# HGRN-2 stage of a hybrid decoder step on one core: projection units placed between the small matrix steps, v in three parts, forget gate and logarithms further forward

## The reference, cut to what matters

```
q, f, v, gate = jnp.split(x @ w_in, 4, axis=-1)
forget = lb + (1.0 - lb) * jax.nn.sigmoid(f)
log_f = jnp.log(forget)
k = (1.0 - lb) * jax.nn.sigmoid(-f)
q = jax.nn.silu(q)
# for each chunk of 16 steps and each of 16 heads:
G = jnp.cumsum(gc, axis=1)
qg = qc * jnp.exp(G)
att = einsum('blhd,bshd->bhls', qg, kc * jnp.exp(-G)), causal
o = einsum('bhls,bshv->blhv', att, vc) + einsum('blhd,bhdv->blhv', qg, S)
S = S * jnp.exp(g_last)[..., None] + einsum('bshd,bshv->bhdv', kc * jnp.exp(g_last - G), vc)
# then
o = rms_norm over the head, * norm_g * silu(gate);  y = o @ w_out
```

## Time and profile before

| what | value |
|---|---|
| median of 3 runs | 2430.7 us (2428.47 to 2439.7) |
| the profiled execution | 2442.74 us |
| its span, first to last instruction | 2440.8 us |
| PE busy | 2236.6 us, 92% of the span |
| DVE, ACT, POOL busy | 1270.4, 982.4, 1247.6 us |
| chain that ended last | PE 64%, DVE 18%, DMA 6%, ACT 5% |
| mean granted TensorE clock | 0.896 |
| stretch of groups i = 1 to 7 of HGRN | 1249.31 to 1692.28 us, 63.3 us a group |

### The profile page before, as it was taken

The page is one execution under the profiler, slowest core; times in us unless marked ns, Lnnn a source line. Parts: engine busy times, 40 slices in busy tenths (PEclk is TensorE's granted clock), DMA queues, the critical chain, the costliest instruction groups (busy, mean ns, idle before and its releaser), DMA issues.

```text
span 2440.8 us, 37825 instructions
## 1 busy us (share of the span) xinstructions
PE 2236.6 (92%) x14852; PEld 2017.3 (83%) x14852; DVE 1270.4 (52%) x2173; ACT 982.4 (40%) x1585; POOL 1247.6 (51%) x1565
## 2 busy tenths in 40 slices
PE   6898998789999999898899999999899889989987
PEld 5888996688899987796698889888799579889966
DVE  5798334146666674434245555555324338982342
ACT  3677432423344432342433322332243247764422
POOL 4798880343344442580363333444386049988702
PEclk8999999878899997899898888888799899999998
DMA  3434466233333323366223333332456624445660
GB/s 110 149 119 130 167 206 215 71 109 108 91 114 119 109 90 107 111 219 230 85 83 106 106 106 95 100 104 85 129 173 198 217 79 133 133 131 170 194 233 31
DMA packets 329760, 321.35 MB, mean 132 GB/s; under 512 B 21512, under 2 KB 311216, under 8 KB 329584
## 3 DMA queue, kind: packets, MB, share of 16 engines
q1 hardware_dynamic: 328720, 318.60, 41.1%
q10 hardware_dynamic: 864, 0.34, 0.1%
HBM read 289.27 MB, written 29.61 MB: 131 GB/s over the span
## 4 chain that ended last, share of the span: by engine, by line
PE 64%; DVE 18%; DMA 6%; ACT 5%; issue 3%; POOL 1%; SPq 1%; ACTq 0%; DVEq 0%
PE ps L669 10%; PE ps L670 9%; PE ps L674 9%; PE ps L1200 4%; PE ps L659 3%; PE ps L679 3%; PE ps L660 2%; PE ps L661 2%; PE ps L1076 2%; DMA work<-cache_mem_v 2%; PE ps L1246 2%; DVE work L2064 2%; PE ps L937 2%; DVE work L1914 2%; PE ps L946 2%
## 5 line engine op out<-in xcount | busy, mean ns | idle before, releaser
L1396 POOL TENSOR_TENSOR wl<-raw,wh 128x256 fp32r<-128x256 f32 x1536 | 1243.1, 846 | 1158.1 <-ACT wh L1419 1157.0
L669 PE MATMUL ps<-Hh,wh 128*128 128x320 f32 (+1 forms) x1536 | 490.2, 335 | 57.4 <-DVE Hl L1960 26.5
L1419 ACT ACTIVATE wh<-raw 128x1024 fp32r<-128x1024 f32 (+1 forms) x400 | 400.2, 1021 | 335.4 <-DMA raw<-hg_w_in 86.6
L670 PE MATMUL ps<-Hl,wh 128*128 128x320 f32 (+1 forms) x1536 | 474.6, 325 | 0.0
L669 PEld LDWEIGHTS ps<-Hh,wh 128*128 128x128 f32 x1536 | 317.2, 207 | 82.0 <-issue 48.2
L670 PEld LDWEIGHTS ps<-Hl,wh 128*128 128x128 f32 x1536 | 318.6, 207 | 1.3
L1914 DVE TENSOR_SCALAR work<-ps 128x512 f32<-128x512 f32 (+9 forms) x248 | 116.1, 486 | 276.0 <-PE ps L1092 56.2
L674 PE MATMUL ps<-Hh,wl 128*128 128x320 f32 (+1 forms) x1536 | 255.3, 309 | 2.5 <-POOL wl L1396 2.5
L674 PEld LDWEIGHTS ps<-Hh,wl 128*128 128x128 f32 x1536 | 234.1, 194 | 3.6 <-POOL wl L1396 3.6
L659 PE MATMUL ps<-Oh,wh 128*128 128x320 f32 x512 | 168.5, 329 | 8.4 <-POOL wl L1396 4.1
L669 PE MATMUL ps<-Oh,wh 128*128 128x320 f32 x512 | 161.4, 328 | 3.7 <-DVE Ol L2607 3.7
(11 more groups left out here) (398 smaller groups left out, 4127.4 us busy)
## 6 DMA issues: line engine op xcount, KB each, us to landing
raw<-rg_w_in SPq DMA_DIRECT2D x128, 256.0 KB, 3.7
work<-cache_mem_k SPq DMA_DIRECT2D x64, 512.0 KB, 4.8
work<-cache_mem_v SPq DMA_DIRECT2D x64, 512.0 KB, 5.9
raw<-hg_w_in SPq DMA_DIRECT2D x128, 256.0 KB, 5.0
raw<-ssd_w_in SPq DMA_DIRECT2D x96, 256.0 KB, 3.8
raw<-rg_w_out SPq DMA_DIRECT2D x64, 256.0 KB, 3.6
raw<-x_w_k SPq DMA_DIRECT2D x64, 256.0 KB, 3.6
raw<-x_w_v SPq DMA_DIRECT2D x64, 256.0 KB, 5.3
```

The costliest lines, as they stand in the source:

```text
L669: pe.matmul(ps[:, bank, 0:n], high(half, k), mh[:, k, 0:n], start=(k == 0), stop=False)
L670: pe.matmul(ps[:, bank, 0:n], high(half, k), ml[:, k, 0:n], start=False, stop=False)
L1396: ins = pool.tensor_tensor(out, src, wh[:, n % HALVES, r:r + 2].bitcast(F32), ALU.subtract)
L1419: act.activation(wh[:, n % HALVES, 0:rows], raw[:, slot, 0:rows, half * P:(half + 1) * P], ACT.Copy).then_inc(hi_ready, 1)
```

## The change

PE's loop for i = 1 to 7 is written anew; the steps of the last pass (i = 8) keep their order. The two units of f are taken apart and stand on either side of `outputs(j, 0)`, ahead of `turn_and_score(j, 1)`. v is taken in three parts, behind `gain(j, 0, 1)`, `gain(j, 1, 0)` and `outputs(j, 1)`. On ACT the copy `s1_copy(j, 1)` goes behind the logarithm and behind the splits of the next group's g units. On DVE `forget(i)` goes ahead of `turned(j, 1)`, and `sums_of_logs(i)` ahead of `last_state(j, 1)`. No instruction is added or removed, and POOL's and SP's lists are the same.

```diff
-                def take_f(i):
+                def take_f(i, half):
                     pe.wait_ge(*past("hg_g_read", i + 1))
-                    project(gfv(i), 0)
-                    project(gfv(i) + 1, 1)
-
-                def take_v(i):
-                    pe.wait_ge(*past("hg_f_read", i + 1))
-                    halves(2)
+                    project(gfv(i) + half, half)
+
+                def take_v(i, T):
+                    if T == 0:
+                        pe.wait_ge(*past("hg_f_read", i + 1))
+                        halves(2)
                     both, rest_of = pair(), pair_low()
...
-                    done(mm, 2)
+                    if T == 2:
+                        done(mm, 2)
...
-                for i in range(1, GROUPS + 1):
-                    last = i == GROUPS
...
-                        take_g(i)
-                        take_q(i, 0)
-                    turn_and_score(i - 1, 0)
...
-                        take_q(i, 1)
-                    states(i - 1, 0)
-                    gain(i - 1, 0, 0)
-                    outputs(i - 1, 0)
-                    turn_and_score(i - 1, 1)
-                    gain(i - 1, 0, 1)
...
-                        take_f(i)
-                    states(i - 1, 1)
-                    gain(i - 1, 1, 0)
-                    outputs(i - 1, 1)
-                    if not last:
-                        take_v(i)
-                    gain(i - 1, 1, 1)
-                    sums(i - 1)
+                for i in range(1, GROUPS):
+                    j = i - 1
+                    take_g(i)
+                    take_q(i, 0)
+                    turn_and_score(j, 0)
+                    take_q(i, 1)
+                    states(j, 0)
+                    gain(j, 0, 0)
+                    take_f(i, 0)
+                    outputs(j, 0)
+                    take_f(i, 1)
+                    turn_and_score(j, 1)
+                    gain(j, 0, 1)
+                    take_v(i, 0)
+                    states(j, 1)
+                    gain(j, 1, 0)
+                    take_v(i, 1)
+                    outputs(j, 1)
+                    take_v(i, 2)
+                    gain(j, 1, 1)
+                    sums(j)
...
                     act.activation(hg_k, ps[:, a:a + 2, 0:NT], ACT.Sigmoid, scale=-1.0).then_inc(S("hg_f_read"), 1)
-                    if i:
-                        s1_copy(i - 1, 1)
                     act.preload_act_table_set(EXP_SET)
                     act.wait_ge(*past("hg_forget", i + 1))
                     act.activation(hg_f, hg_f, ACT.Ln).then_inc(S("hg_logf"), 1)
                     ahead(b + 6)
+                    if i:
+                        s1_copy(i - 1, 1)
                     act.wait_ge(*past("hg_G_ready", i + 1))
...
+                    if i < GROUPS:
+                        forget(i)
+                    if i:
                         turned(i - 1, 1)
                         new_state(i - 1, 0, 1)
                         blocks_of_v(i - 1, 1)
                     if i < GROUPS:
-                        forget(i)
+                        sums_of_logs(i)
                     if i:
                         last_state(i - 1, 1)
-                    if i < GROUPS:
-                        sums_of_logs(i)
-                    if i:
                         gated(i - 1, 1)
                         new_state(i - 1, 1, 0)
```

More of the change, by code:

```diff
@@ L1040, in take_q @@
                     project(qs(i) + half, half)
-                def take_f(i):
+                def take_f(i, half):
                     pe.wait_ge(*past("hg_g_read", i + 1))
-                    project(gfv(i), 0)
-                    project(gfv(i) + 1, 1)
-                def take_v(i):
-                    pe.wait_ge(*past("hg_f_read", i + 1))
-                    halves(2)
-                    both, rest_of = pair(), pair_low()
[L1051 to L1056, removed]
-                    done(mm, 2)
+                    project(gfv(i) + half, half)
[3 more added lines that the diff above has]
+                        halves(2)
+                    both, rest_of = pair(), pair_low()
+                    t0 = (0, P, NT - P)[T]
+                    out = ps[:, gfv(i) + T // 2, 256 * (T % 2):256 * (T % 2) + 256]
+                    for k in range(KD):
+                        for n, (x, w) in enumerate(((Hh, both), (Hh, rest_of), (Hl, both))):
+                            mm = pe.matmul(out, x[:, k, t0:t0 + P], w(k), start=(k == 0 and n == 0), stop=(k == KD - 1 and n == 2))
+                    if T == 2:
+                        done(mm, 2)
                 def turn_and_score(i, h):
@@ new lines, in hg @@
+                take_f(0, 0)
+                take_f(0, 1)
+                for T in range(3):
+                    take_v(0, T)
+                for i in range(1, GROUPS):
[19 more added lines that the diff above has]
+                    sums(j)
@@ new lines, in hg @@
+                pe.wait_ge(*past("hg_q_read", GROUPS))
+                take_out(0, 0)
+                take_out(0, 1)
+                turn_and_score(7, 0)
+                pe.wait_ge(*past("hg_v_read", GROUPS))
+                take_out(0, 2)
+                states(7, 0)
+                gain(7, 0, 0)
+                outputs(7, 0)
+                turn_and_score(7, 1)
+                gain(7, 0, 1)
+                take_out(0, 3)
+                states(7, 1)
+                gain(7, 1, 0)
@@ L1164, in hg @@
+                outputs(7, 1)
+                gain(7, 1, 1)
+                sums(7)
                 pe.wait_ge(*past("hg_o_read", GROUPS * 2))
```

14 lines of the change are left out of this document (removed).

## The result

| | before | after |
|---|---|---|
| median (range), us | 2435.2 (2428.47 to 2441.24) | 2478.14 (2469.12 to 2479.4) |
| profiled execution, us; span | 2442.7; 2440.8 | 2476.97; 2475.1 |
| groups 1 to 7, a group | 63.28 us | 67.83 us |

The changed kernel is slower: the ratio is 1.0149, with a 95% interval of 1.0117 to 1.018. The two sides were run in turn on one chip, so its median of before is not quite that of the table ahead of the prediction. The span of the profiled execution grew by 34.3 us, and 31.8 of them lie in groups 1 to 7.

A forecast was written before the change was run, and what follows sets the result against it. PE, busy 92% of the span, was taken as the bound, through waits and stretches at 1.2 GHz. 38.5 + 28.7 = 67.2 us a group against 63.28, times seven 27 us more: 2458 us, range 2434 to 2490.

The forecast's parts named there:

- The mechanism: Before head 1's outputs PE idles 6 to 9 us for ACT's copy behind two splits; outputs then run at clock 0.50.
- The DMA chain: SP's head 0 state store, next load and g block: 10.9 us from store to ACT's first split.
- Second part: Group from head 0's second gain to its end: 16.0 + 5.6 + 5.1 + 2.0 = 28.7 us, bounds 26.2 and 31.
- First part: Group up to head 0's second gain, now with all of f: 38.5 us, bounds 36.2 to 43.
- the clock behind the outputs of head 0: Loss in the f unit after head 0's outputs: 0.8 us taken, between 0 and 1.64.
- the clock within `turn_and_score(j, 1)`: Clock loss inside head 1's scores step: 0.7 us taken, between 0 and 4.7.
- The sum: Groups 1 to 7: 67.2 us each against 63.28, 3.9 more, times seven 27 us; forecast 2458, chance 0.65.
- the clock stays down: Rival, much slower: first part 42.5, second 29.5, 72.0 us a group, +61 us, 2492; chance 0.13.
- The counts of nothing: Waits on the f block (at most 1.5 us), the keys and head 0's copy counted at 0, as covered.
- The wait isn't met: Rival, faster: g block lands before PE reaches head 1's outputs; group 55.9 us, time 2379; chance 0.07.
- point of no gain: Second part: no gain and no loss if head 1's copy came at +12 instead of +16.
- The clock pays for the wait: Rival, no change: clock held throughout first part (36.2), back within outputs (27.0); 63.2 us a group, 2430; chance 0.15.

The follow-up runs named there:

- Run 4: Kernel before, only ACT's copy of head 1 moved behind the logarithm and the two splits; 2466.23 us, ratio 1.0114.
- run 3: Changed kernel, with SP loading the next group's g and q blocks ahead of head 0's state store and load; 2401.07 us, ratio 0.9857.
- run 5: Changed kernel, with ACT's two g splits moved behind head 1's copy and the square of its outputs; 2420.88 us, ratio 0.9918.
- run 6: Changed kernel, with g and q blocks ahead of head 0's store on SP and the copy ahead of the splits on ACT; 2405.72 us, ratio 0.9867.
- run 7: Changed kernel, ACT's splits behind copy and square, SP's g, q and f blocks ahead of the state stores; 2392.54 us, ratio 0.9799.
- Run 1: Changed kernel, with ACT's copy of head 1 moved right behind the logarithm, ahead of the two splits; 2449.05 us, ratio 1.0043.
- run 11: Kernel with splits moved and blocks loaded early, but both f units together ahead of head 0's outputs; 2411.0 us, ratio 0.9895.

## Why the prediction was right, and where it was off

**The mechanism** was as described: in all seven groups PE stands before head 1's outputs for 6.3 to 8.1 us (predicted 6 to 9), ended by ACT's copy behind two splits, the first of which ended a wait for `raw`. The outputs behind it took 5.63 us at 0.50 in each of them. Run 4 shows that the copy's place alone brings this wait, also in the old order, and run 3 that an earlier g block takes it away.

**The DMA chain.** From store to split the prediction took 10.9 us; it was 10.98 in group 4 and 10.29 to 12.18 over the seven groups, 10.9 in the mean. The rule cited there ("DMA: Bandwidth & Descriptors" of the Trainium skill, "Anatomy of one DMA") gave 8.8, and no group of the changed kernel was that fast. The page gives this fit for DMAs that gpsimd issues, which the prediction left out; here SP issues them. For the store the trace agrees with it all the same, 3.2 us by the rule and 3.23 from 1497.94 to 1501.17; the gap is in the load and the block behind it, 5.6 by the rule and 7.75 from 1501.17 to 1508.92.

**Second part.** 28.49 us against 28.7. Its terms: outputs 5.63 at 0.50 (5.6), and, in group 4, the last third of v 5.40 (5.1), gain and sums 2.19 (2.0), and outputs that start at +16.06 (+16.0). Over the seven groups v is 4.88 and gain and sums 2.02.

**First part.** 39.34 us against 38.5. Two terms were guesses between bounds, and one of them was mis-sized: the clock behind the outputs of head 0. The prediction took 0.8 of at most 1.64 us; the unit of f behind them took 5.14 us in six of seven groups, that is 1.6 more than at full clock, and 3.60 in the seventh. The other guess, 0.7 us for the clock within `turn_and_score(j, 1)`, erred the other way: the step kept full clock in six groups, and with its gain lost 0.4 us in the mean. The rest is that `turn_and_score(j, 0)` and the q unit were slower in groups 2, 3 and 6.

**The sum.** 67.83 us a group against 67.2, 31.8 us over seven groups against 27. The measured ratio makes 36 us, the prediction's 27. Of the span's growth 2.5 us lie outside groups 1 to 7, where the prediction had counted nothing: group 1 starts 5.9 us later, and the time behind the groups is 3.5 us shorter. Both are within what the profiled executions differ by there, so that these 2.5 us say nothing of the change.

**Slips in the working**, none of which moved the forecast: the lower bound of the first part, 36.2, lies below the sum of its own terms, 36.99; the upper bound of the second part comes to 31.9 with the terms named, not 31; the rival "the clock stays down" names 1.5 us for f, which its 42.5 does not hold; and the landing at +13.5 in group 3 is group 7's, as the split began at +14.2 in group 3 (1428.73 against 1414.49).

**The counts of nothing.** The f block, the keys and the copy of head 0 made no wait, as said. For f this held only in a long group: at 60.83 us (run 5) the same chain was late by 5.4 us. It was a cover by the length of the group: the prediction's 7.1 us between head 1's outputs and the next g hold the slow v behind the wait, and in run 5 they are 5.0.

**The rivals.** "The wait isn't met" named the right price: 55.9 us a group, and 56.9, 56.7 and 56.1 were measured in runs 3, 6 and 7. But the road to it was described too narrowly. The prediction followed the copy only, and from its terms a copy ahead of the splits would have been that case. Run 1 shows that it isn't: the square of head 1's outputs stands behind the same splits, and PE's last gain behind that, through DVE. What had to be asked is all that stands behind the waiting instruction in ACT's list, not just the instruction that was moved. For the same reason the "point of no gain" at a copy at +12 describes a case that moving the copy cannot give. "The clock pays for the wait" and "the clock stays down" did not come about: the first part lay between them, at 39.34 (36.2 and 42.5), and the clock was not back within the outputs.

## What to carry to other kernels

An instruction that waits for a transfer holds everything behind it on its engine. Before a step is moved behind one, list all that stands there and who waits for it; when the first victim is freed, the second shows. An order that is right for the matrix engine can lose to one transfer's place in a queue: here weight blocks that depended on nothing stood behind a store and a load that depended on the computation. Taking them ahead gained 11 us a group in the new order and nothing in the old, where the block was on no path. And a gain in one part shortens the cover of every chain that has a fixed length. Test such a reorder with that wait removed before judging it: this one cost 1.5% as it stood and was 2% faster than before with two blocks loaded earlier and two splits moved.

## What the runs showed of the hardware

Short steps can cost the clock of the step behind them, here behind the outputs of one head. Run 7, group 4: outputs of head 0, the unit of f behind them, `turn_and_score(j, 1)`, gain, first third of v:

```profile
1452.33:1455.26 2.93, 2.93 (x27) 1.00 0.99 313
1455.26:1460.39 5.13, 5.13 (x26) 0.67 0.00 1
1460.39:1464.55 4.16, 4.16 (x40) 1.00 0.02 4
1464.55:1465.60 1.05, 1.05 (x5) 1.00 0.00 0
1465.60:1470.06 4.46, 4.46 (x25) 0.62 0.13 42
```

The small steps themselves run at 2.4 GHz, and the dense one behind them pays: 5.13 us instead of 3.52, 4.46 instead of 2.87, 1.6 us each time, behind 2.93 us of small work as behind 5.21. But it is no fixed price. The same outputs and the same unit of f in group 2 of the same execution:

```profile
1341.24:1344.17 2.93, 2.93 (x26) 1.00 1.10 348
1344.17:1347.77 3.60, 3.60 (x26) 1.00 0.18 57
```

In run 7 this unit pays in groups 1, 4 and 7 and not in the other four, in the changed kernel it pays in six of seven, in run 5 in none. What decides it was not found. What the rows do bear out is that a dense step ahead of `turn_and_score(j, 1)` mostly keeps that step fast: 4.16 us in all seven groups of run 7 and in six of the changed kernel (5.19 in group 6). Right behind the outputs it took 7.06 to 7.86 us in the kernel before and 5.2 to 7.5 us in run 11.

The store of the prompt's state, 128 KB, mostly costs nothing beside the store of 512 KB ahead of it: both land in 3.2 us in the median of the changed kernel's seven groups, and the next load starts 3.7 us behind the first store. At times it does: in group 4 of run 5, shown above, that load starts 5.3 us behind the store, in one more group of that run 5.1 and in one of the changed kernel 5.5. The reason was not found.
